# A streaming-encoder block on one core: ada's first blocks summed by GpSimd and VectorE, dummy products in TensorE's waits, the last squares summed by TensorE, and the relative-bias table written with other access patterns

## What is computed

```python
mod = silu(c) @ ada_w + ada_b            # 1024 -> 9 * 1024
sh1, sc1, g1, sh2, sc2, g2, sh3, sc3, g3 = split(mod, 9)
h = rms_norm(x, norm_ffn1) * (1 + sc1) + sh1
x = x + 0.5 * g1 * ((silu(h @ w_gate) * (h @ w_up)) @ w_down)
h = rms_norm(x, norm_mix) * (1 + sc2) + sh2
x = x + g2 * token_mixing(h)             # two attention branches; one adds rel_bias[clip(t - s)]
h = rms_norm(x, norm_ffn2) * (1 + sc3) + sh3
x = x + 0.5 * g3 * ((silu(h @ w_gate2) * (h @ w_up2)) @ w_down2)
return rms_norm(x, final_norm)
```

## Time and profile before

| | |
|---|---|
| median of 3 runs | 1204.09 us (1203.87 to 1204.37) |
| the profiled execution | 1201.57 us, of which the span is 1199.9 us |
| TensorE, matmul busy | 1155.1 us, 96% of the span |
| VectorE / ScalarE / GpSimd busy | 52% / 40% / 4% |
| mean granted TensorE clock | 0.975 |

### The profile page before, as it was taken

The page is one execution under the profiler, slowest core; times in us unless marked ns, Lnnn a source line. Parts: engine busy times, 40 slices in busy tenths (PEclk is TensorE's granted clock), DMA queues, the critical chain, the costliest instruction groups (busy, mean ns, idle before and its releaser), DMA issues.

```text
span 1199.9 us, 15312 instructions
## 1 busy us (share of the span) xinstructions
PE 1155.1 (96%) x5278; PEld 956.1 (80%) x5278; DVE 618.9 (52%) x1004; ACT 475.7 (40%) x708; POOL 42.0 (4%) x70
## 2 busy tenths in 40 slices
PE   6999899999999989999999999997999999999997
PEld 4888677888888867888888888885888888888885
DVE  5565466666555557655645666746333333333332
ACT  5032232323222237555645656534343444332222
POOL 0001100000000011100001110000000000000000
PEclk8799899999999989999999999998999999999999
DMA  9446665566555424333234542331333333333332
GB/s 315 143 141 205 208 189 169 192 201 201 162 168 168 133 53 131 107 88 88 70 104 103 127 114 71 91 101 38 105 103 93 99 92 100 96 92 97 96 96 83
DMA packets 224582, 151.09 MB, mean 126 GB/s; under 512 B 8583, under 2 KB 206421, under 8 KB 224549
## 3 DMA queue, kind: packets, MB, share of 16 engines
q1 hardware_dynamic: 217252, 139.02, 38.9%
q0 software_dynamic: 6720, 9.55, 3.1%
q10 hardware_dynamic: 576, 2.10, 0.5%
HBM read 148.47 MB, written 4.25 MB: 127 GB/s over the span
## 4 chain that ended last, share of the span: by engine, by line
PE 47%; issue 42%; DMA 5%; SPq 2%; DVE 2%; ACT 2%; POOL 0%; DVEq 0%; POOLq 0%; ACTq 0%
PE bank L1199 13%; PE bank L1200 13%; PE bank L1201 13%; DMA raw<-in_ffn_w_gate_dram 4%; PE bank L1399 1%; SPq L392 1%; ACT wH L543 1%; PE bank L1228 1%; PE bank L1387 1%; PE bank L1392 1%; PE bank L1415 1%; PE bank L1414 1%; DMA adas<-in_ada_w_dram 1%; SPq L411 1%; SPq L405 0%
## 5 line engine op out<-in xcount | busy, mean ns | idle before, releaser
L1199 PE MATMUL bank<-hH,wH 128*128 128x512 f32 x1080 | 428.8, 397 | 9.4 <-DVE hL L861 8.1
L1200 PE MATMUL bank<-hL,wH 128*128 128x512 f32 x1080 | 424.0, 393 | 0.0
L1201 PE MATMUL bank<-hH,wL 128*128 128x512 f32 x1080 | 423.8, 392 | 0.0
L543 ACT ACTIVATE wH<-raw 128x1024 fp32r<-128x1024 f32 (+1 forms) x187 | 194.7, 1041 | 541.9 <-PE bank L1201 510.2
L782 DVE TENSOR_TENSOR wL<-raw,wH 128x1024 fp32r<-128x1024 f32 (+1 forms) x187 | 224.7, 1202 | 327.6 <-ACT wH L543 326.9
L1199 PEld LDWEIGHTS bank<-hH,wH 128*128 128x128 f32 x1080 | 205.0, 190 | 56.9 <-issue 11.4
L1201 PEld LDWEIGHTS bank<-hH,wL 128*128 128x128 f32 x1080 | 204.9, 190 | 43.6
L1200 PEld LDWEIGHTS bank<-hL,wH 128*128 128x128 f32 x1080 | 205.2, 190 | 41.4
L1199 PE MATMUL bank<-actH,wH 128*128 128x512 f32 x352 | 137.1, 389 | 0.0
L1201 PE MATMUL bank<-actH,wL 128*128 128x512 f32 x352 | 137.0, 389 | 0.0
L1200 PE MATMUL bank<-actL,wH 128*128 128x512 f32 x352 | 136.9, 389 | 0.0
(11 more groups left out here) (158 smaller groups left out, 911.3 us busy)
## 6 DMA issues: line engine op xcount, KB each, us to landing
adaw<-in_ada_w_dram SPq DMA_DIRECT2D x28, 1024.0 KB, 6.1
raw<-in_ffn_w_gate_dram SPq DMA_DIRECT2D x43, 512.0 KB, 3.8
raw<-in_ffn_w_up_dram SPq DMA_DIRECT2D x43, 512.0 KB, 3.8
raw<-in_mix_w_in_dram SPq DMA_DIRECT2D x41, 512.0 KB, 3.8
raw<-in_ffn_w_down_dram SPq DMA_DIRECT2D x32, 512.0 KB, 3.7
adas<-in_ada_w_dram SPq DMA_DIRECT2D x16, 512.0 KB, 8.4
raw<-in_ffn_w_down_dram SPq DMA_DIRECT2D x16, 384.0 KB, 3.4
raw<-in_mix_w_out_dram SPq DMA_DIRECT2D x8, 512.0 KB, 3.7
```

What stands on the lines that cost most here:

```text
L543: nc.scalar.activation(wH[s][:, :n * P], raw[s][:, :n * P], ACT.Copy).then_inc(hi_done, 1)
L1199: T.matmul(o, a[0], b[0], start=start, stop=False)
L1200: T.matmul(o, a[0], b[1], start=False, stop=False)
L1201: return T.matmul(o, a[1], b[0], start=False, stop=stop)
```

## The change

GpSimd takes rows 0 to 2 of each of the first four blocks (a scaled row, then twice scale and add, into adasp), VectorE takes rows 3 to 7 and keeps its running sum in a PSUM bank until the last row. TensorE's first_parts is gone; first_sums makes 16 records instead of 8, the first 8 after GpSimd's part and the last 8 after VectorE's. It also waits for xt_done. The order of tiles in first_units is changed, and dummies (now 128x256, bfloat16, on ident) are issued in more places: 44 instead of 16 at first, 12 and 8 around spread(0), 24 and 20 in first_units, 14 ahead of spread(1) and spread(2) and 18 behind each. The eighth square is not added by VectorE: token_squares does four products with ssqa once seven are in, waits for ScalarE's last square and adds four products with that. The relative-bias table goes over a further table in DRAM, rels_d, of 8 heads by 16 rows, and the transfers are written with 32 outer rows of 8. The last iterations of down(0) and of the output projection stand outside their loops.

```diff
-    ROWS_V = (7, 6, 5, 4)
+    ROWS_P = 3
-    DUMMIES = 16
+    DUMMIES = 44
...
+            def first_rows(b):
+                pool.wait_ge(adas_in[b][0], 32)
+
+                nc.gpsimd.tensor_scalar(adasp[:, b, :], adas[:, b, 0, :], csilu[:, 0:1], None, ALU.mult).then_inc(adasp_step, 1)
+                for k in range(1, ROWS_P):
+                    scaled = sqx[:, 0:AC] if k % 2 else sqx[:, AC:]
+                    pool.wait_ge(adasp_step, (b * ROWS_P + k) * 2 - 1 - b)
+                    nc.gpsimd.tensor_scalar(scaled, adas[:, b, k, :], csilu[:, k:k + 1], None, ALU.mult).then_inc(adasp_step, 1)
+                    pool.wait_ge(adasp_step, (b * ROWS_P + k) * 2 - b)
+                    nc.gpsimd.tensor_tensor(adasp[:, b, :], scaled, adasp[:, b, :], ALU.add).then_inc(adasp_step, 1)
...
+                pool.dma_start(rels_d[:, :, 0:SEQ + 7], bass.AP(relx_d.tensor, P - 7, [[SEQ + P, HB], [-8, 16], [1, SEQ + 7]])
+                               ).then_inc(rels_out, 16)
+                pool.wait_ge(rels_out, 16)
...
-                skewed = bass.AP(relx_d.tensor, P + 2 * i * (SEQ + P), [[SEQ + P, 2], [-1, P], [1, SEQ]])
-                pool.dma_start(relb_d[2 * i:2 * i + 2, :, :], skewed).then_inc(relb_out, 16)
+                skewed = bass.AP(rels_d.tensor, 2 * i * 16 * (SEQ + 8) + 7, [[SEQ + 8, 32], [-1, 8], [1, SEQ]])
+                pool.dma_start(relb_d[2 * i:2 * i + 2, :, :].rearrange("h (a b) s -> (h a) b s", b=8), skewed).then_inc(relb_out, 16)
...
                 if n == 0:
-                    first_rows(0, 4, ROWS_V[0])
+                    first_rows(0, 4, DT)
...
-                            first_rows(b, 0, ROWS_V[b])
+                            first_rows(b, ROWS_P, DT)
...
             def first_rows(b, k0, k1):
+                acc = bank[:, B_ACC, :]
...
             def add_squares(m, j, i):
+                if isinstance(i, int) and 2 * i + j == DT - 1:
+                    return
...
+                for n in range(2 * AC // P):
+                    if n == 0:
+                        pe.wait_ge(adasp_step, (b + 1) * (2 * ROWS_P - 1))
+                    if n == AC // P:
+                        pe.wait_ge(adas_step, (b + 1) * (DT - ROWS_P))
...
+                dummies(24)
                 tiles(0, 0)
                 tiles(1, 0)
-                first_parts(1)
                 first_sums(1)
-                first_parts(2)
+                dummies(20)
                 tiles(0, 1)
                 tiles(1, 1)
+                tiles(2, 0)
+                tiles(2, 1)
                 first_sums(2)
-                first_parts(3)
-                for u in (2, 3):
-                    tiles(u, 0)
-                    tiles(u, 1)
+                tiles(3, 0)
+                tiles(3, 1)
                 tiles(0, 2)
+                tiles(1, 2)
                 first_sums(3)
-                for u in range(1, N_FIRST):
-                    tiles(u, 2)
+                tiles(2, 2)
+                tiles(3, 2)
...
-                pe.wait_ge(ssqa_done[m], DT + START)
+                pe.wait_ge(ssqa_done[m], DT - 1 + START)
                 for t in range(TT):
-                    ins = T.matmul(bank[:, B_SSQ, t:t + 1], ssqa[:, t * P:(t + 1) * P], ones[:, 0:1], start=True, stop=True)
+                    T.matmul(bank[:, B_SSQ, t:t + 1], ssqa[:, t * P:(t + 1) * P], ones[:, 0:1], start=t == 0, stop=False)
+                pe.wait_ge(sq_done[m], DT)
+                for t in range(TT):
+                    ins = T.matmul(bank[:, B_SSQ, t:t + 1], tmp[:, 1, t * P:(t + 1) * P], ones[:, 0:1], start=False, stop=t == TT - 1)
...
             def spread(n):
+                if n:
+                    dummies(14)
                 pe.wait_ge(diag_done, n + 1)
...
+                if n:
+                    dummies(18)
...
+            dummies(12)
             spread(0)
-            pe.wait_ge(c_act, 1)
-            first_parts(0)
+            dummies(8)
             pe.wait_ge(onesr_made, 1)
+            pe.wait_ge(xt_done, DT)
             first_sums(0)
```

More of the change, by code:

```diff
@@ L158, in hybrid_block @@
             adasc = sb("adasc", [P, ADA0, AC], stack=at_start)
+            adasp = sb("adasp", [P, ADA0, AC], stack=at_start)
         in_ffn = ExitStack()
@@ L208, in hybrid_block @@
         B_ADA, B_BC, B_SSQ, B_FA = 4, 4, 7, 7
+        B_IDLE = 3
         B_LAST = 5
-        B_ADA_START = (3, 5, 6, 7)
+        B_ADA_START = (5, 6, 5, 6)
+        B_ACC = 7
         XT_BANK = (1, 2, 5, 6)
-        B_DUMMY = 7
         Y_BANK = ((0, 1, 2, 3), (4, 5, 6, 0))
@@ L219, in hybrid_block @@
         negF_d = nc.dram_tensor("negF_d", [HA, SEQ], F32, kind="Internal").ap()
+        rels_d = nc.dram_tensor("rels_d", [HB, 16, SEQ + 8], F32, kind="Internal").ap()
         relx_d = nc.dram_tensor("relx_d", [HB, SEQ + P], F32, kind="Internal").ap()
@@ L243, in hybrid_block @@
         adas_step = sem("adas_step")
+        adasp_step = sem("adasp_step")
         adas_sum = sem("adas_sum")
@@ L282, in hybrid_block @@
         relx_out = sem("relx_out")
+        rels_out = sem("rels_out")
         relb_out = sem("relb_out")
@@ L495, in _ @@
                 if n == 0:
+                    for b in range(ADA0):
+                        first_rows(b)
                     pool.wait_ge(pow_done, 1)
@@ L977, in body @@
                     for k in range(6):
-                        if ada and isinstance(i, int) and k == 2:
+                        if ada and isinstance(i, int) and i == 0 and k == 2:
                             columns()
@@ L989, in down @@
                     body(0)
-                with dve.Fori(int(ada), DT // 2 - n) as i:
+                with dve.Fori(int(ada), DT // 2 - 1) as i:
                     body(i)
-                if n == 1:
-                    body(DT // 2 - 1)
+                body(DT // 2 - 1)
             def forget_sums():
@@ L1174, in _, with out_projection @@
             branch(1)
-            with dve.Fori(0, DT // 2) as i:
+            def out_projection(i):
                 for k in range(2):
@@ L1179, in _ @@
                     add_squares(1, k, i)
+            with dve.Fori(0, DT // 2 - 1) as i:
+                out_projection(i)
+            out_projection(DT // 2 - 1)
             normed(2)
@@ L1220, in h_unit @@
                 return dense(u, s, o, h, ks, ks[0] == 0, ks[-1] == DT - 1, ks[0])
-            def first_parts(b):
-                for q in range(2):
-                    pe.wait_ge(adas_in[b][q], 32)
-                for n in range(AC // P):
-                    for r in range(ROWS_V[b], DT):
-                        T.matmul(bank[:, B_ADA_START[b], 4 + n:5 + n], adas[:, b, r, n * P:(n + 1) * P],
-                                 csilu[:, r:r + 1], start=r == ROWS_V[b], stop=r == DT - 1)
-            def first_sums(b):
-                pe.wait_ge(adas_step, sum(ROWS_V[:b + 1]))
-                for n in range(AC // P):
-                    ins = T.matmul(bank[:, B_ADA_START[b], n:n + 1], adasc[:, b, n * P:(n + 1) * P], ones[:, 0:1],
+            def first_sums(b):
+                for n in range(2 * AC // P):
[3 more added lines that the diff above has]
+                        pe.wait_ge(adas_step, (b + 1) * (DT - ROWS_P))
+                    cols = slice(n % (AC // P) * P, (n % (AC // P) + 1) * P)
+                    ins = T.matmul(bank[:, B_ADA_START[b], n:n + 1], (adasp, adasc)[n // (AC // P)][:, b, cols], ones[:, 0:1],
                                    start=True, stop=True)
```

26 lines of the change are left out of this document (12 added, 14 removed).

## The result

| | before | after |
|---|---|---|
| median | 1204.23 us | 1185.9 us (1185.24 to 1187.16, 4 runs) |
| ratio | | 0.9846 (95%: 0.9829 to 0.9863) |
| profiled execution, its span | 1201.57, 1199.9 us | 1185.24, 1183.6 us |
| mean granted clock | 0.975 | 0.991 |

Faster by 18.3 us where 21.3 were forecast; from one profiled execution to the other it is 16.3 us. The time is inside the range, 3.1 us above the forecast.

A forecast was written before the change was run, and what follows sets the result against it. TensorE, busy 96% of the span, was the bound, so only its waits and half-clock times could shrink: -9.9 - 11.2 - 1.6 + 1.3 + 0.1 = -21.3 us, a median of 1182.8, range 1177 to 1190.

The forecast's parts named there:

- The start: Kernel's opening up to the first unit behind it: to end at 60.0 us instead of 69.89, a gain of 9.9 us.
- I take 5.5 us and no cost: Block 0 of the opening: GpSimd's five steps take 5.5 us, within 5 to 7, and delay nothing.
- the third rival: Opening: VectorE holds off GpSimd, which becomes the bound; costs from 1.76 us a step, 1211.6 us at 3.2; chance 0.02.
- GpSimd's steps: Opening, each block: three single-input steps and two with two inputs, together 5 to 7 us, taken as 5.5.
- The rows and the hand-over of VectorE's chain: Opening, each block: VectorE's five rows take 3.6 us, TensorE's sum behind the last row 0.9 with the hand-over.
- The table: Relative-bias table transfers during gate_up(0): spread over sixteen engines they land in 2 to 4 us, gaining 11.2 us.
- The second rival: gate_up(0): table transfers on all engines still stall it, gain 6 instead of 11.2 us, time 1188.0; chance 0.10.
- normed(2): The second norm: earlier sum of squares and a spread partly at full clock, 1.6 us less, bounds 0.9 and 2.3.
- normed(1): The first norm: dummies at half clock ahead of the spread make it 1.3 us longer, bounds -1.3 and +2.
- The end: Kernel's end behind the transposes: 16 records instead of 8 before the mean, +0.1 us, within 0.3 either way.
- The first: Rival for the opening: GpSimd's first block 2 us late and half clock, gain only 6 us, time 1186.7; chance 0.20.

## Why the prediction was right, and where it was off

- **The start: -4.8 instead of -9.9.** This is the term that was mis-sized by much. By the columns of each block, measured against forecast: block 0 at 24.16 instead of 21.5 (+2.7); the way to block 1 11.06 instead of 9.2 (+1.9), to block 2 12.40 instead of 10.3 (+2.1), to block 3 8.66 instead of 8.0 (+0.7); from there to the first unit 8.80 instead of 11.0 (-2.2), since nearly all of the 2.5 us that the forecast had added for half clock were not spent there. The step that failed is "I take 5.5 us and no cost" for GpSimd. I had read the shared interface as a danger to GpSimd alone (the third rival), and priced VectorE's weight parts and hL from the earlier trace rows, where GpSimd is silent. The runs put 4.0 us on VectorE held up and 0.5 to 2 on GpSimd late, the latter with the clock's part in it.
- **GpSimd's steps.** Forecast 5.5 us for five; measured 1.59 + 1.56 + 1.30 + 1.56 + 1.26 and the gaps, 7.6 us. The upper end of 7 was too low, as 0.50 us for 256 columns was of another instruction. Block 0 was done at 21.6, 1.1 us behind VectorE's part of it, and TensorE waited 2.20 us. My estimate of 1.1 us for the two-input add was near (1.26 to 1.30); that a scaled row takes longer than an add I had not foreseen.
- **The rows and the hand-over of VectorE's chain.** In the run without GpSimd five rows take 3.98 us in blocks 1 to 3, forecast 3.6: the prediction took the same price for the sum in PSUM, and the scaled row into PSUM is 0.75 instead of 0.48. From the end of the last row to the columns it is 1.49, 1.14 and 1.14 us, forecast 0.9. Together they make the last columns 1.8 us late, and the shorter tail (9.7 instead of 11.0) hid most of it. In the changed kernel block 0's sixteen records took 2.4 us at falling clock.
- **The table: -11.5 in the profile, -10.7 alone by the medians; forecast -11.2.** Right, with its reason: engines, not bytes. The transfers land after 3.8, 6.4, 6.1 and 6.2 us instead of 2 to 4, and the copy after 3.5 instead of 2, still under what was covered. The second rival is out.
- **normed(2): -1.9; forecast -1.6.** Right as described: the 8 records of spread(2) take 1.12 us, and at most 1.25 in nine other profiles with this order.
- **normed(1): +1.9 in the profile, +2.1 on average; forecast +1.3**, upper bound 2. The direction and the mechanism (dummies at half clock ahead of the spread) were right; that the clock can fall at different moments, which moves the length between 11.98 and 15.24 us, was not in it. Five of the ten profiles lie beyond the upper bound.
- **The end: +0.1**, as forecast.
- **The sum.** -4.8 - 11.5 + 1.9 - 1.9 + 0.1 = -16.2, measured 16.3 between the profiled executions. The medians are 18.3 apart, since the profiled run of before was 2.7 us below its median and that of after 0.7. The terms miss by 5.1 us; that the medians miss by 3.1 only is chance.
- **The rivals.** The first named the outcome best (its 1186.7 is 0.8 off) and had half of its reason: GpSimd's block was late, but in the changed kernel's profile the clock was granted in most of the start, and the larger part came over VectorE. The third had the sharing, at the wrong engine: GpSimd's steps stayed under its price of 1.76 but for three, of 1.88, 1.86 and 3.59 us.

## What to carry to other kernels

Work given to GpSimd isn't free for VectorE: count, on VectorE's path, each instruction with two SBUF inputs that runs beside it, and keep one of the inputs (an accumulator above all) in PSUM; the first row written there cost 0.27 us more here. When a step leaves an engine, ask who becomes late next: fewer rows for GpSimd in block 0 only moved the wait to block 1, where the data's landing set it, and TensorE in GpSimd's place lost the same to its clock. A DRAM to DRAM transfer like this one wants an outer size of 8 or more, and a stage made of one-column products should be timed in several profiles before a variant is judged by it.

## What the runs showed of the hardware

- Beside GpSimd, VectorE's subtraction of 128x1024 with both inputs in SBUF takes 2.27 to 2.32 us instead of 1.22, a multiply-add of 128x512 up to 1.33 instead of 0.78; with one input in PSUM it stays at 0.75. A scaled row of 128x512 from SBUF to SBUF took 0.83 once instead of 0.48; into PSUM it takes 0.75 with or without GpSimd. GpSimd is held up in turn: its scaled row at 40.15 us took 3.59 instead of 1.56 and ended at 43.74, 1.4 us behind the end of VectorE's pair of weight parts at 42.39, which is about its own length. The Trainium skill, "SBUF — State Buffer", section "Who interferes with whom", says that a VectorE instruction with two SBUF inputs contends with a GpSimd instruction that reads SBUF, that the port pair they share is an exclusive lock, and that the order of issue decides who is blocked. The traces agree: the later one waits for the other's end (the weight part of 20.41 ends 1.1 us behind GpSimd's add, which ends at 21.59), and instructions with an operand in PSUM are not held up.
- GpSimd takes 1.56 us to scale 128x512 by a per-partition factor and 1.27 to add two such tiles.
- TensorE's granted clock falls from 1.00 to 0.50 (2.4 to 1.2 GHz) while it is busy without a gap, when what it does is one-column products: in the runs with a long normed(1), 16 records took 1.84 us at first and 3.55 a few microseconds later.
- 512 KB from DRAM to DRAM land after 16.0, 11.1, 7.1 and 6.4 us with 2, 4, 8 and 16 outer rows, and after 3.8 to 7.3 with 32, most of them beside weight transfers.
